# An adaLN layer with sliding-window attention and a gated recurrence: the attention output turned earlier, x tiles normalised earlier, the last mixing tile in another order

## The reference

```
mod = silu(c) @ w_ada + b_ada                       # 6 x 1024 a row of c
h   = rmsnorm(x, ln1) * (1 + sc1) + sh1
qa, ka, va, qb, fb, ib, gb = split(h @ w_in)        # 1024 -> 2816
oa  = windowed GQA attention of qa, ka, va with sinks and ALiBi    # 512 columns
ob  = rmsnorm(gated recurrence of qb, fb, ib) * silu(gb)           # 512 columns
x   = x + g1 * (concat(oa, ob) @ w_out)
h2  = rmsnorm(x, ln2) * (1 + sc2) + sh2
x   = x + g2 * moe(h2)                              # 16 experts, the router in fp32, 2 experts a token
```

## Time and profile before

| | |
|---|---|
| median of 3 runs | 1388.79 us (1384.99 to 1390.72) |
| profiled execution | 1390.75 us, its span 1388.7 us |
| busy, share of the span | PE 87%, PEld 73%, DVE 53%, ACT 40%, POOL 27% |
| mean granted TensorE clock | 0.919 of full |
| projection, group "i" | about 44 to 113 us of the span |
| mixing | about 431 to 807 us of the span |
| route and experts | about 808 us to the end |

### The profile page before, as it was taken

One profiled execution on the slowest core, in us unless ns is written; L12 is line 12 of the kernel. 1 busy time (PEld: TensorE's weight loads), 2 busy tenths in 40 slices (PEclk: granted clock), 3 DMA queues, 4 the chain that ended last, 5 costly groups with the idle time before them and its releaser, 6 DMA issues. The chain is left out here.

```text
span 1388.7 us, 21648 instructions
## 1 busy us (share of the span) xinstructions
PE 1213.9 (87%) x7081; PEld 1007.5 (73%) x7082; DVE 735.8 (53%) x1066; ACT 550.5 (40%) x921; POOL 370.5 (27%) x419
## 2 busy tenths in 40 slices
PE   4689999999497999999999726999999999879964
PEld 1568889988465887888888625888887887768853
DVE  1653411342544666666665365562565585756762
ACT  1653411323333445445443204442343465444640
POOL 1001200122503434344442102232323331433313
PEclk9899999999766999799997857999999999989987
DMA  9626673412276232321230175486759889787874
GB/s 349 231 93 220 238 280 119 155 51 71 65 209 159 81 93 83 104 80 65 92 95 24 50 263 193 153 269 210 247 168 333 279 282 361 252 291 257 271 270 91
DMA packets 119430, 249.87 MB, mean 180 GB/s; under 512 B 17713, under 2 KB 47153, under 8 KB 116290
## 3 DMA queue, kind: packets, MB, share of 16 engines
q1 hardware_dynamic: 107266, 204.92, 42.6%
q0 software_dynamic: 12096, 44.05, 12.0%
HBM read 205.02 MB, written 43.93 MB: 179 GB/s over the span
## 5 line engine op out<-in xcount | busy, mean ns | idle before, releaser
L2125 PE MATMUL psum<-e_w_h,e_x_h 128*128 128x512 f32 x432 | 174.3, 404 | 30.7 <-DVE w_gu L2238 24.1
L2127 PE MATMUL psum<-e_w_h,e_x_l 128*128 128x512 f32 x432 | 171.1, 396 | 0.0
L2126 PE MATMUL psum<-w_gu,e_x_h 128*128 x432 | 171.1, 396 | 0.0
L2072 POOL DMA_INDIRECT out<-e_work,e_to x26 | 87.9, 3380 | 299.8 <-DVE e_work L2226 299.8
L2238 DVE TENSOR_TENSOR w_gu<-w_gu,e_w_h 128x1024 f32 x128 | 146.7, 1217 | 21.8 <-ACT e_w_h L2179 21.8
L2179 ACT ACTIVATE e_w_h<-w_gu 128x1024 fp32r x128 | 123.0, 1048 | 53.8 <-issue 32.0
L2125 PEld LDWEIGHTS psum<-e_w_h,e_x_h 128*128 128x128 f32 x432 | 82.9, 192 | 49.0 <-DVE w_gu L2238 24.5
L499 PE MATMUL psum<-p_w_h,p_h_h 128*128 128x512 f32 (+1 forms) x288 | 105.7, 367 | 0.0
L500 PE MATMUL psum<-p_w_l,p_h_h 128*128 128x512 f32 (+1 forms) x288 | 105.0, 364 | 0.0
L501 PE MATMUL psum<-p_w_h,p_h_l 128*128 128x512 f32 (+1 forms) x288 | 104.9, 364 | 0.0
L2127 PEld LDWEIGHTS psum<-e_w_h,e_x_l 128*128 128x128 f32 x432 | 82.8, 192 | 18.0
(11 more groups left out here) (382 smaller groups left out, 2616.0 us busy)
## 6 DMA issues: line engine op xcount, KB each, us to landing
w_gu<-in_w_e_gate SPq DMA_DIRECT2D x16, 2048.0 KB, 10.8
w_gu<-in_w_e_up SPq DMA_DIRECT2D x16, 2048.0 KB, 15.4
w_dn<-in_w_e_down SPq DMA_DIRECT2D x16, 2048.0 KB, 15.0
shared<-in_w_ada SPq DMA_DIRECT2D x24, 1024.0 KB, 6.4
p_w_raw<-in_w_in SPq DMA_DIRECT2D x5, 2048.0 KB, 9.4
tok_d<-p_tok SPq DMA_DIRECT2D x27, 256.0 KB, 2.0
feat_d<-p_work SPq DMA_DIRECT2D x12, 576.0 KB, 3.4
p_work<-in_x SPq DMA_DIRECT2D x9, 512.0 KB, 3.8
```

The costliest lines, as they stand in the source:

```text
L2072: pool.indirect_dma_start(out=d["y"], out_offset=bass.IndirectOffsetOnAxis(ap=to_now[1 - par][:, 0:1], axis=0), in_=y_s[:, 1 - par, :], in ...
L2125: pe.matmul(psum[:, j, :], x_h[:, k, :], wh, start=(k == 0), stop=False)
L2126: pe.matmul(psum[:, j, :], x_h[:, k, :], wl, start=False, stop=False)
L2127: last = pe.matmul(psum[:, j, :], x_l[:, k, :], wh, start=False, stop=(k == KC - 1))
```

## The change

Three edits. (1) In projection `load_x(1)` is issued ahead of the first weights, `norm(1)` stands ahead of the first splits on ACT, and in the loop `norm(i + 2)` stands ahead of keep_h(i + 1) and the split. (2) In mixing o_a is turned into bank OB right behind the turn of q and k, its copy and high part follow on ACT ahead of the square of ob, and `rest(t + 1, 0)` stands ahead of `residual(t)` on DVE. The matmuls of the recurrence's output now wait for the copy of o_a (`mixa_ready`). (3) In the last unit PE runs fills 0 and 1, the turn of ob, fill 2, the turn of h2, fill 3, the logits of unit 7, and fills 4 to 7; DVE runs `residual(8)` ahead of `keep_logits(7)`, and makes the product of `weigh(8)` itself, which POOL no longer does.

```diff
--- before.py
+++ after.py
@@ -334,8 +334,8 @@
                 sp.dma_start(ln1_t[:, :], ln1.rearrange("(k p) -> p k", p=P)).then_inc(s["ln_loaded"], 16)
             for i in range(STAGES, KC):
                 load_stage(i)
+            load_x(1)
             load_w(0)
-            load_x(1)
             sp.dma_start(o_norm_w[:, :], o_norm.partition_broadcast(P)).then_inc(s["consts_loaded"], 16)
             for n, src in enumerate((q_norm, k_norm)):
                 sp.dma_start(norm_w[:, n, :], src.partition_broadcast(P)).then_inc(s["consts_loaded"], 16)
@@ -540,20 +540,20 @@
 
             act.wait_ge(s["eps_made"], 1)
             norm(0)
+            norm(1)
             for part in range(4):
                 split(0, part)
             keep_h(0)
-            norm(1)
             for n, (g, i) in enumerate(JOBS):
                 name = GROUPS[g][0]
                 out = tok[:, tok_use(n) % TOK_RING, :]
                 if name == "i":
+                    if i + 2 < NT:
+                        norm(i + 2)
                     if i + 1 < NT:
                         keep_h(i + 1)
                     if after_job(n) is not None:
                         split(after_job(n), n - FIRST_JOB[g] - 2)
-                    if i + 2 < NT:
-                        norm(i + 2)
                 act.wait_ge(s["job_done"], n + 1)
                 if name in ("i", "q"):
                     if tok_stores_before(n):
@@ -1298,7 +1298,6 @@
                 for i in range(3, NL):
                     make_gap(t, i)
             weigh(NU - 2)
-            weigh(NU - 1)
 
         @block.tensor
         def _(pe):
@@ -1438,6 +1437,8 @@
                 if t + 1 < TP:
                     turn_qk(t + 1)
                 pe.wait_ge(s["kdt_ready"], t + 1)
+                pe.wait_ge(s["oa_ready"], t + 1)
+                turn4(OB, o_a[:, :, :, :].rearrange("p g k d -> p (g k d)"), s["oa_turned"])
                 pe.wait_ge(s["pair_ready"], (t + 1) * NL)
                 i_b = toks(t, TOK_I, QW)
                 for h in range(8):
@@ -1446,7 +1447,7 @@
                                      kd_tok[:, h * HD:(h + 1) * HD], i_b[:, h * HD:(h + 1) * HD], start=True, stop=True)
                 last.then_inc(s["state_mm"], 1)
                 fill(t, 7, t + 1 if t + 1 < TP else None)
-                pe.wait_ge(s["oa_ready"], t + 1)
+                pe.wait_ge(s["mixa_ready"], t + 1)
                 pe.wait_ge(s["qe_ready"], t + 1)
                 pe.wait_ge(s["state_ready"], t + 1)
                 for h in range(8):
@@ -1460,17 +1461,17 @@
                                      start=False, stop=True, skip_group_check=True)
                     if h >= 6:
                         last.then_inc(s["ob_mm"], 1)
-                pe.wait_ge(s["x1_ready"], t + 1)
-                turn4(W0, o_a[:, :, :, :].rearrange("p g k d -> p (g k d)"), s["oa_turned"])
             u = NU - 1
-            for k in range(4):
-                fill(u, k)
+            fill(u, 0)
+            fill(u, 1)
             turn_ob(TP - 1)
+            fill(u, 2)
             pe.wait_ge(s["mixb_ready"], TP)
             turn_h2(u - 1)
+            fill(u, 3)
+            logits(u - 1)
             for k in range(4, KC):
                 fill(u, k)
-            logits(u - 1)
             pe.wait_ge(s["logit_ready"], u)
             turn_h2(u)
             logits(u)
@@ -1569,11 +1570,11 @@
                 a(kd_tok[:, :], psum[:, OB, :], ACT.Copy).then_inc(s["kdt_ready"], 1)
                 if t + 1 < TP:
                     keep_qk(t + 1)
+                act.wait_ge(s["oa_turned"], t + 1)
+                a(mixed(t + 1, 0), f4(psum[:, OB, :]), ACT.Copy).then_inc(s["mixa_ready"], 1)
+                high(t + 1, 0)
                 act.wait_ge(s["ob_mm"], t * 2 + 2)
                 a(o_sq.rearrange("p (a c) d -> p a (c d)", a=2), psum[:, OA:OA + 2, 0:4 * HD], ACT.Square).then_inc(s["osq_ready"], 1)
-                act.wait_ge(s["oa_turned"], t + 1)
-                a(mixed(t + 1, 0), f4(psum[:, W0, :]), ACT.Copy).then_inc(s["mixa_ready"], 1)
-                high(t + 1, 0)
                 act.wait_ge(s["oss_ready"], t + 1)
                 olink = Chain(act, s["o_rs"], 2 * t)
                 olink(a(o_rs[:, :], o_ss[:, :], ACT.Ln, scale=1.0 / HD, bias=eps[:, :]))
@@ -1729,6 +1730,7 @@
                 dve.tensor_tensor(o_a[:, :, :, :], psum[:, OA, :].rearrange("p (g k d) -> p g k d", g=G, d=HD),
                                   bc(rec[:, :, :].rearrange("p k g -> p g k"), 3, HD), ALU.mult).then_inc(s["oa_ready"], 1)
                 place(t, 6)
+                rest(t + 1, 0)
                 residual(t)
                 dve.wait_ge(s["ob_mm"], 2 * t + 2)
                 link(dve.tensor_tensor(state[:, :, :], state[:, :, :],
@@ -1737,13 +1739,14 @@
                                   ALU.add).then_inc(s["state_ready"], 1)
                 dve.wait_ge(s["osq_ready"], t + 1)
                 dve.tensor_reduce(o_ss[:, :], o_sq[:, :, :], AX_X, ALU.add).then_inc(s["oss_ready"], 1)
-                rest(t + 1, 0)
             heads_normed(TP - 1)
             u = NU - 1
             normed(u - 1)
             rest(u, 1)
+            residual(u)
             keep_logits(u - 1)
-            residual(u)
+            dve.wait_ge(s["x2_ready"], u + 1)
+            dve.tensor_tensor(xw[:, :], x2[:, u % 2, :], table_row(2, u), ALU.mult).then_inc(s["xw_ready"], 1)
             normed(u)
             keep_logits(u)
 
```

## The result

The changed kernel took 1384.03 us (median of 20 runs, 1378.23 to 1392.66), the kernel before 1394.27 us (20 runs, 1383.53 to 1405.76). The ratio is 0.9941, 95% interval 0.9919 to 0.9963: some 8 us faster. That is inside the predicted range (1377 to 1394 us), and above the size forecast: -3.2 us of 1388.8 is a ratio of 0.9977. The 20 runs of before have their median 5.5 us above that of the three runs that were shown, so the ratio, not the absolute time, is to be held against the forecast. On the 1388.79 us of those three runs it gives 1380.6 us: inside the range of 1377 to 1394, and just under the narrower forecast of 1381.5 to 1389.5.

What follows compares the result with a forecast made beforehand. PE was taken to bound the kernel, so a gain could only be one of its waits or its clock. Edits of +3.8, -0.5 and -6.5 sum to -3.2 us on the 1388.79 us median: 1385.6 us, range 1377 to 1394.

Steps and rivals of the forecast that it cites:

- the narrower forecast: Whole kernel: the time forecast to fall between 1381.5 and 1389.5 us, with a chance of 0.53.
- the loop: Projection, group "i" on ACT: copy to copy 9.27 us against 8.49, with iteration 1 costing 0.9, 4.8 us lost in all.
- The flight: Projection: time from SP's issue of a load of x until it lands, taken as 3.6 us.
- The head start: Start of projection: norm(1) runs while the weights are in flight, so the first copy comes 1.3 us earlier.
- the weights' delay: Start of projection: load_x(1) ahead in the queue delays the 2 MB of weights by some 1.2 us.
- the boundary waits are not won, the lock takes them: Mixing tile boundaries: POOL's running instruction holds DVE's decayed(0) in place of rest; about -0.5 us, not 7.6 us won.
- Nothing is removed: Mixing tile boundaries, edit 2: the change takes no work away; about -0.5 us forecast.
- the +0.23 us for each boundary from tile 2 to 6: Mixing: tops comes 0.27 us sooner after the reduce, itself 0.5 late; five boundaries cost +1.2 us together.
- a milder clock: Rival, mixing: shorter boundary waits spare one spell of low clock, -7 us, giving 1378.6 us; chance 0.12.
- a change in their number: Mixing: if the count of low-clock spells changes, the prediction is wrong.
- The boundary waits are simply won: Rival, mixing tile boundaries: the lock does not matter, -7.6 us instead of -0.5, giving 1378.5 us; chance 0.14.
- Group "i" at half clock: Rival, projection: jobs at 1.2 GHz take 12.2 us; all six cost 17 us, giving 1403 us; chance 0.06.
- Edit 1 gains as it reads: Rival, projection: x_normed no longer stops PE, up to 11 us gained; chance 0.04.

Runs made afterwards that it cites:

- weigh_behind_tops: The changed kernel with each load of x issued one job earlier and POOL's weigh moved behind DVE's tops; ratio 0.9751 to the kernel before.

## Why the prediction was right, and where it was not

**The total: right, in part by luck.** -3.2 us was forecast and about -8 measured, inside the range. Two terms missed in opposite directions: edit 1 cost more than its +3.8 us, and mixing from tile 0 to 7 gained 8.6 where 0.5 was forecast. The two partly cancel, and with edit 1 as forecast the total would have been near the fast end of the range.

**Edit 1: right in sign and mechanism, the size about half of it.** +3.8 us was forecast; against the profile of before it is +7.3 in the first trace and +5.5 to +7.3 in the four that have it with the loads as they are. The mis-sized term is the loop: 4.8 us over six iterations were forecast, 6.3 are read (from the first copy to the seventh 49.13 us before and 55.45 after). The flight was taken at 3.6, the low side of 3.5 to 3.8, and was 3.6 to 4.0, and iteration 1 cost 1.0. The head start of 1.3 us was nothing in the changed kernel's profile (the first copy at 51.85 against 51.31) and 0.4 to 0.9 in three others. The step that failed there is the weights' delay: ACT's first split starts at 37.21 us against 34.91, so they came 2.3 us later and not 1.2, and the first job started at 43.36 instead of the 42.2 that was worked out (44.21 before). Then TensorE ran it at half clock until 48.65 us, where before it was at full clock from 46.91 on.

```profile
37.21 3.89 ACT L539 ACTIVATE p_w_h<-p_w_raw 128x1024 fp32r<-128x1024 f32 x4 [2.55 <-DMA p_w_raw<-in_w_in]
...
43.36 0.79 PE L499 MATMUL psum<-p_w_h,p_h_h 128*128 128x512 f32 x1 [4.71 <-DVE p_h_l L655]
...
51.85 0.60 ACT L563 ACTIVATE p_tok<-psum 128x512 f32<-128x512 f32 x1 [0.61 <-PE psum L501]
```

That the order on ACT was sound and only the loads late, the two kernels with early loads show.

**Edit 2: the step "the boundary waits are not won, the lock takes them" was right; "Nothing is removed", as the whole of it, was the wrong step.** `decayed(0)` was held 1.55 us as forecast. Structure was forecast at -0.5 us and is about -2.5. The sign at the first two boundaries was right, and their size was -1.2 each instead of -0.8; the step that failed is the +0.23 us for each boundary from tile 2 to 6, which were 0.1 us shorter or the same (39.1 against 39.2 or 39.1 at full clock). What the forecast put into a rival with a chance of 0.12, a milder clock, -7 us, came true in about that size: some -6.1 us. The forecast counted spells, and named a change in their number as a sign of being wrong. Before and after there are six in these seven tiles, but two of 13.7 us are gone and one of 10.2 came, and the time at half clock fell from 41.0 to 27.3 us. It had the boundary's order and the clock's spells as two things with separate chances; the experiments show that a change of that order changes the spells, and not by which rule.

**Edit 3: the sum right, the owner wrong.** -7.1 worked out, -6.5 forecast, -7.5 measured. But 6.2 of these belong to edit 2, which takes the 2.72 us wait and the half clock behind it away; the order of edit 3 and the product on DVE add 1.2 (2.3 when alone). The forecast's text booked them under edit 3 since it took the state after edit 2 as given.

**The rivals.** "The boundary waits are simply won" is out: 39.1 us between boundaries at full clock, not 38.4. Group "i" at half clock did not happen: 0.96 mean clock from 47 to 120 us in the changed kernel, with the loss at its start and in one short stretch (0.61 from 80 to 84 us) that left the loop at 9.45 us, since ACT and the load set it. "Edit 1 gains as it reads" was out for the reason given, SP's order, and comes true once that order is changed.

The steps as read sum to +7.3 - 8.6 - 7.5 = -8.8 us, and to -10.0 at the last logits with 1.2 us that went between group "i" and tile 0; the ratio of 0.9941 is -8.2 us.

## What to carry to other kernels

A wait that is taken away is worth what is next in line: work out what the freed engine will wait for instead, and for DVE and GpSimd look which two-input instructions will now fall under a running GpSimd instruction, small ones too. Before an instruction is moved ahead of others on its engine, check when its input's DMA is issued: the order pays only if the load is moved by the same step. Where TensorE's clock stands below 1.00 in the windows, compare the time at half clock between the two kernels, stretch by stretch, before any gain is put down to structure, and read an edit of half a percent from places in several traces beside the timed ratio.

## What was not expected of the hardware

The clock's spells in mixing repeat with the instruction pattern: about 285.5 us and 27.3 us at half clock in five different kernels whose first boundary came anywhere from 465 to 483 us, 294.1 and 41.0 in three, though in two of the seven executions the longest spell came one tile later. A kernel with hardly a wait left at its boundaries (weigh_behind_tops) had 41.0 us at half clock all the same. They also spread: the timed runs of before, and of the kernels with the old boundary, ranged over 15 to 25 us, and over 50 runs of before beside two of the trials their time follows their mean clock with a correlation of -0.85. A GpSimd tensor_tensor of 2.4 us held a DVE instruction on 128x4 elements for 2.23 us.
